# Joining the score and value steps of attention on one Trainium2 core, and slowing their pace

## What is computed

```python
q = (h @ w_q).reshape(B, n_c, CHUNK, B_HEADS, B_HEAD_DIM)
s = jnp.einsum('bnqhd,bnkhd->bnhqk', q, k_band) * (B_HEAD_DIM ** -0.5) + bias
s = jnp.where(valid, s, -jnp.inf)
p = jax.nn.softmax(s, axis=-1)
o = jnp.einsum('bnhqk,bnkhd->bnqhd', p, v_band).reshape(B, S, B_HEADS * B_HEAD_DIM)
y = o @ w_o
```

## Time and profile before

| | |
|---|---|
| median of 3 runs | 972.28 us (971.98 to 974.05) |
| span of the profiled execution | 971.6 us |
| TensorE busy | 953.6 us (98%) |
| VectorE busy | 715.1 us (74%) |
| ScalarE busy | 544.0 us (56%) |
| attention of layer 1, and of layer 2 | about 336 to 394 us, and 645 to 722 us |

### The profile page before, as it was taken

How to read it: one execution, slowest core, us unless ns; L and a number is a source line. 1 busy time by engine, 2 the same in 40 slices (tenths; PEclk the granted TensorE clock), 3 DMA queues, 4 the chain that set the end, 5 groups by cost and what they waited for, 6 DMA issues and landing times.

```text
span 971.6 us, 18766 instructions
## 1 busy us (share of the span) xinstructions
PE 953.6 (98%) x7909; PEld 919.1 (95%) x7909; DVE 715.1 (74%) x1326; ACT 544.0 (56%) x845; POOL 17.7 (2%) x51
## 2 busy tenths in 40 slices
PE   9999999999999999999999999999999999999997
PEld 9889999999998988899999997998999999999997
DVE  7875897786669777798788898556655889888653
ACT  7755654444447366655444555456755566666542
POOL 0000000000000000000000000000320000000000
PEclk9999999999999999999999999999999999999999
DMA  9646286667646634177768881653333536565621
GB/s 345 228 161 238 91 327 233 237 241 275 246 131 223 255 131 166 53 281 275 268 240 300 306 325 58 246 174 130 129 132 131 209 139 216 178 208 180 217 87 44
DMA packets 28259, 195.62 MB, mean 201 GB/s; under 512 B 3216, under 2 KB 3600, under 8 KB 5264
## 3 DMA queue, kind: packets, MB, share of 16 engines
q1 hardware_dynamic: 28176, 194.43, 56.3%
HBM read 192.98 MB, written 1.05 MB: 200 GB/s over the span
## 4 chain that ended last, share of the span: by engine, by line
PE 87%; ACT 6%; DVE 4%; issue 2%; DMA 1%; SPq 0%; POOL 0%; DVEq 0%; ACTq 0%
PE bank L539 25%; PE bank L540 24%; PE bank L545 23%; ACT s_whi L986 2%; PE bank L715 2%; PE bank L741 2%; PE bank L624 2%; PE bank L618 2%; PE bank L619 2%; PE bank L583 1%; PE bank L590 1%; DVE s_wlo L1474 1%; PE bank L584 1%; PE bank L725 1%; DMA s_front<-in_front 1%
## 5 line engine op out<-in xcount | busy, mean ns | idle before, releaser
L1474 DVE TENSOR_TENSOR s_wlo<-s_raw,s_whi 128x512 fp32r<-128x512 f32 (+1 forms) x354 | 364.4, 1070 | 136.6 <-ACT s_whi L986 136.3
L986 ACT ACTIVATE s_whi<-s_raw 128x1024 fp32r<-128x1024 f32 (+2 forms) x226 | 299.6, 1352 | 206.0 <-PE bank L545 197.7
L539 PE MATMUL bank<-s_hh,s_whi 128*128 128x256 f32 x1392 | 391.5, 281 | 2.0 <-DVE s_wlo L1474 1.7
L540 PE MATMUL bank<-s_hl,s_whi 128*128 128x256 f32 x1392 | 385.6, 277 | 0.0
L545 PE MATMUL bank<-s_hh,s_wlo 128*128 128x256 f32 x1375 | 380.8, 277 | 0.0
L539 PEld LDWEIGHTS bank<-s_hh,s_whi 128*128 128x128 f32 x1392 | 262.1, 188 | 8.3 <-issue 6.2
L540 PEld LDWEIGHTS bank<-s_hl,s_whi 128*128 128x128 f32 x1392 | 261.5, 188 | 0.1
L545 PEld LDWEIGHTS bank<-s_hh,s_wlo 128*128 128x128 f32 x1375 | 258.2, 188 | 0.0
L539 PE MATMUL bank<-s_ph,s_whi 128*128 128x256 f32 x528 | 146.4, 277 | 0.0
L540 PE MATMUL bank<-s_pl,s_whi 128*128 128x256 f32 x528 | 145.8, 276 | 0.0
L545 PE MATMUL bank<-s_ph,s_wlo 128*128 128x256 f32 x516 | 142.5, 276 | 0.0
(11 more groups left out here) (256 smaller groups left out, 1299.2 us busy)
## 6 DMA issues: line engine op xcount, KB each, us to landing
s_raw<-in_gu SPq DMA_DIRECT2D x44, 1024.0 KB, 4.8
s_raw<-in_dn SPq DMA_DIRECT2D x33, 1024.0 KB, 4.9
s_raw<-in_wada SPq DMA_DIRECT2D x24, 1024.0 KB, 5.1
s_raw<-in_up SPq DMA_DIRECT2D x22, 1024.0 KB, 4.9
s_raw<-in_wo SPq DMA_DIRECT2D x8, 1024.0 KB, 4.9
s_raw<-in_win_g SPq DMA_DIRECT2D x8, 1024.0 KB, 4.8
s_raw<-in_mla SPq DMA_DIRECT2D x4, 1024.0 KB, 13.6
s_raw<-in_wkv_v SPq DMA_DIRECT2D x4, 1024.0 KB, 5.6
```

Source lines behind the costliest of these rows:

```text
L539: e.matmul(out, hi, xh[:, k, :], start=first, stop=False, skip_group_check=True)
L540: e.matmul(out, hi, xl[:, k, :], start=False, stop=False, skip_group_check=True)
L986: e.activation(whi[w % SPLIT][:, at], src, ACT.Copy).then_inc(S.hi.tick((w, c0)), 1)
L1474: e.tensor_tensor(wlo[s][:, at], src, whi[s][:, at].bitcast(F32), ALU.subtract).then_inc(S.lo.tick((i, j), (i, "all")), 1)
```

## The change

The table `beside` lets a `values` step follow directly on `scores` (and `sticks` on `values`) at the same product step, without a credit and whatever the credit is, if its distance is kept. The paces of layers 1 and 2 are lowered from 0.35 to 0.28 and from 0.3 and 0.2 to 0.24 and 0.16. Layer 0 keeps its order. No instruction is added or taken away.

```diff
--- before.py
+++ after.py
@@ -152,6 +152,7 @@
 
 
     steps, ahead, at, made, credit = iter(steps), [], {}, set(), 0.0
+    beside = {"values": "scores", "sticks": "values"}
 
     def peek():
         if not ahead:
@@ -187,9 +188,11 @@
         yield unit
         at[unit] = n
         credit = min(credit + paces[unit[0]], 2.0)
-        while peek() is not None and (credit >= 1 or ahead[0][0] in FREE) and ready(n):
-            if ahead[0][0] not in FREE:
+        latest = None
+        while peek() is not None and (credit >= 1 or ahead[0][0] in FREE or beside.get(ahead[0][0], 0) == latest) and ready(n):
+            if ahead[0][0] not in FREE and beside.get(ahead[0][0], 0) != latest:
                 credit -= 1
+            latest = ahead[0][0]
             yield taken(n)
     while peek() is not None:
         yield taken(len(units))
@@ -215,13 +218,13 @@
 
 
 def _order1():
-    return _mixed(_units("wq1") + _units("wo1"), _soft_steps(range(8)), {"wq1": 0.35, "wo1": 0.35},
+    return _mixed(_units("wq1") + _units("wo1"), _soft_steps(range(8)), {"wq1": 0.28, "wo1": 0.28},
                   lambda p: ("wq1", 16 * (p // 2) + 15), "wo1")
 
 
 def _order2():
     return _mixed(_units("win_q") + _units("win_g"), itertools.chain(_soft_steps(range(4)), _stick_steps(range(4, 8))),
-                  {"win_q": 0.3, "win_g": 0.2}, lambda p: ("win_q", 16 * (p // 2) + 15), None)
+                  {"win_q": 0.24, "win_g": 0.16}, lambda p: ("win_q", 16 * (p // 2) + 15), None)
 
 
 class Signal:
```

## The result

| | before | changed |
|---|---|---|
| median, us (5 runs each) | 973.02 (971.98 to 974.05) | 978.09 (976.88 to 979.92) |
| ratio, 95% interval | | 1.0055 [1.0043, 1.0067] |
| span of the profiled execution | 971.6 | 975.0 |
| TensorE busy | 953.6 us | 950.7 us |

The changed kernel is slower, as forecast, but by 5.1 us and not by 3.6. Its median lies 0.3 us above my range. Every run of both kernels takes 1.9 us more than its span (the profiled execution of the changed kernel: 976.88 and 975.0), so the profiled execution of before was one of about 973.5, above its median.

A forecast was written before the change was run, and what follows sets the result against it. TensorE, busy 98% of the span, was taken to bound the kernel. Layer 1 at +4.1 and layer 2 at -0.5 gave +3.6 us: span 975.2, median 975.9 us (0.7 above the span), range 973.0 to 977.8.

The forecast's parts named there:

- Bound and place: TensorE, busy 98%, bounds the kernel; a loss needs only that it waits; layer 1 +4.1 us, layer 2 -0.5.
- the two releasers that I named: Layer 1: values would wait for ScalarE's copy of the turned scores, turns for VectorE; largest single wait 2.1 us.
- Joins, -1.4: Scores directly followed by values, seven new places in layers 1 and 2: each saves 0.20 us, 1.4 in all.
- The rival of 0.10 each: Scores to values costs as much as other changes, so a join saves 0.10, not 0.20; 976.6 us; chance 5%.
- Pairs 1, 2, 3 and 5: Layer 1, values waiting for ScalarE's second copy: 0.13 us at pair 1, 0.41 each at 2, 3 and 5.
- Pair 4: Layer 1, no weight instruction between its copies: TensorE's way 4.02 against ScalarE's 3.46 us, so no wait.
- Turn into bank 5: First turn of pair 4, layer 1, waits for VectorE to free bank 5 behind its weight parts: 1.8 us.
- Values of pair 6: Layer 1, values wait for ScalarE's second copy behind the 128x2048 weight instruction: 2.1 us, the largest single term.
- Turn of pair 7, 0.65: Layer 1, first turn of pair 7 waits for VectorE's scaling behind its 128x2048 weight part: 0.65 us.
- Waits that go, and layer 2: Layer 1's old chunk and pair 6 waits go, -0.8 us; layer 2 sums to -0.4 + 0.3 - 0.4 = -0.5.
- the term of the sticks: Layer 2, stick-breaking pairs in their new order change by some tenths; bounded by -0.4 and +0.4 us, taken as 0.

The follow-up runs named there:

- the opened pair: Kernel with layer 1's weight parts held back (969.86 us), each of its ten joins opened by one product step; 972.45 us, ratio 0.9992.
- the other execution: The changed kernel run and profiled once more, unaltered; 978.31 us against 972.74, ratio 1.0056.
- select_later: Changed kernel, but GpSimd's 128x2048 affine select waits until VectorE has scaled the scores of pair 7; 976.28 us, ratio 1.0043.
- pair6_clear: Changed kernel, but layer 1 weight parts held only from pair 6's first turn to the scaling of pair 7; 974.1 us, ratio 1.0017.

## Why the forecast was right in kind and wrong in size

- **Bound and place.** Right. The loss is TensorE waiting in layer 1, for the two releasers that I named.
- **Joins, -1.4.** Right: forecast 0.20 each, measured 0.17 to 0.19, and 0.20 by the rows of the opened pair. The rival of 0.10 each is out: scores to values takes 0.86, the same as scores to a product. By the rule of the Trainium skill, TensorEngine Tiling (Array Packing), Key Properties, that the rival was named with, that step is a change of the tiling mode and drains TensorE; no cost of it shows here.
- **Pairs 1, 2, 3 and 5.** Forecast 0.13 and 0.41 three times, measured 0.24 and 0.46 three times. Pair 4 none, as forecast.
- **Turn into bank 5.** Forecast 1.8, measured 1.76, and about 2.6 us come back together with the wait of pair 3 when the parts are held there.
- **Values of pair 6.** Forecast 2.1, measured 2.15.
- **Turn of pair 7, 0.65.** This is the step that failed: measured 2.07 and, in the other execution, 1.84. I had taken the scaling's duration as it stood in before (1.01) and looked at no engine beside VectorE and TensorE. The loss moved VectorE's part and the scaling onto GpSimd's select, which in before took 2.00 us and ran, after its first 0.2, beside an idle VectorE. Under the select the scalings took 2.48, which is 1.47 more; 0.65 + 1.47 = 2.12, against 2.07 measured. With the select out of the way they took 1.01 again.
- **Waits that go, and layer 2.** The two in layer 1 went. Layer 2 came out at -0.9 instead of -0.5. The only wait of over 0.2 for a copy there is 0.24 shown at the values of pair 0, which is 0.30 by starts, as forecast. The rest is the term of the sticks, which I had set at 0 between -0.4 and +0.4: their values waited for GpSimd in before, 0.34 at 712.36 and 0.16 at 692.43 by starts, which my rows of before left out, and both are gone, so the term is -0.5, just outside my bounds. Then -0.4 + 0.3 - 0.35 - 0.5 = -0.95, against -0.91 in the lined-up trace.
- **The clock.** Missing altogether. The wait of 2.1 at the values of pair 6 brings it down in some executions, at a price between nothing and 2.0 us by where the slow stretch falls. No rival had it. My expectations blamed two long waits in a row; the rows show it down ahead of the second, and down in `select_later`, where there is no second. The three runs in which it stayed up lie between 976.88 and 977.90, about the upper end of my range of 977.8, so without the fall of the clock the median would have come out near that end.

The sum of what was seen in layer 1 is -1.0 + 0.24 + 3 x 0.46 + 1.76 + 2.15 + 2.07 - 0.8 = 5.8. The lined-up traces give 5.6 at 406 us and 5.3 at 437, between which before ran some slower stretch. With layer 2 that is 4.4, and the medians say 5.1, the ratios 5.4; the clock that falls in some of the runs is the difference that I can name. Of the 2.2 us between 975.9 and 978.09, 0.7 is that before itself ran at 973.02 in this comparison instead of 972.28; the other 1.5 are the turn of pair 7 (1.4), the short waits (0.3) and the clock, less the better layer 2 (0.4).

## What to carry to other kernels

When attention steps move against weight work, write down for every engine what stands in its queue ahead of the step that TensorE will wait for, and move both halves of a split weight behind it: moving them only behind ScalarE's copies left VectorE's half ahead of its scaling and its scores and handed the delay on (984.7 us), moving them behind the attention work of both engines turned a loss of 5 us into a gain of 2.5. When a forecast moves an instruction in time, look at what the engine beside it runs at the new time, GpSimd beside VectorE above all, and give a new wait of 2 us on TensorE the price of a clock at half speed behind it. Line two traces up instruction by instruction before comparing their spans: here 1.0 of 4.4 us was hidden by differences outside the changed part.

## What the runs showed of the hardware

**TensorE has two paces at full granted clock.** In the stretch from 128 to 143 us, which no change touches, before and the changed kernel run the same products at a granted clock of 1.00 in both, but at distances of 0.118 and 0.113 us. Their windows show 130 and 135 matmuls in 15 us:

```profile
128.00:143.00 15.00, 15.00 (x130) 15.00 (x129) 14.53 (x20) 7.81 (x9) 0.00 (x0) 1.00 0.90 333
```
```profile
128.00:143.00 15.00, 15.00 (x135) 15.00 (x134) 14.67 (x21) 7.98 (x10) 0.00 (x0) 1.00 0.91 327
```

Some stretches are slow in all thirteen profiled executions (84 to 92 us, 732 to 740), others in some (128 to 143 in nine of them, 788 to 804 in five). One such stretch of 15 us costs 0.6. In all some 90 to 170 us of a span are slow, which at 4% is 3.5 to 6.5 us of time and could make up the spread of 2 to 3 us between runs of one kernel; that it does was not shown, and what sets the pace was not tested.

**GpSimd and VectorE hold each other up**, here by 1.9 us on a select of 2.0 and by 1.5 on scalings of 1.0, about as long as the other engine's instruction still ran. Taking the overlap away took both away.

**The granted clock can fall to half behind a single wait of 2.1 us** of TensorE, in some executions and not in others with the same wait. It fell in four of the five profiled executions that have this wait (not in the first one of the changed kernel), in each ahead of the wait that came next, and it was at half for 3.4 to 6.8 us. In the kernels without a wait of 2 us or more, `pair6_clear` with its 1.6 among them, no run that is counted here has a mean clock under 0.998. In the kernel of 984.7 us, which has one wait of 2.4 and one of 4.1, it fell during the second.
